# A two-layer streaming encoder step on one core: phases linked by two alternating semaphore sets instead of meetings, with three orders of filler work changed

## The chip, the core and the metric

The kernel runs on one core of one Trainium2 chip. The metric is the device time of one execution in microseconds (us), as a median of several runs. The engines are named as in the profile: PE is TensorE, ACT is ScalarE, DVE is VectorE, POOL is GpSimd, and SP is SyncE, which issues the DMAs of this kernel. A suffix q (PEq, SPq) is an engine's sequencer, PEld is the weight load of PE.

## What is computed

One inference step of a hybrid streaming encoder: 1024 new frames of one stream and 64 frames of a running stream (1088 tokens together), width 1024, two layers, all in 32-bit floats. Each layer normalizes and modulates its input, projects it once with a wide matrix, and divides the columns among three token mixers and the merge gates:

```
h      = modulate(rmsnorm(x), shift, scale)          # adaLN from c
proj   = h @ w_in                                     # columns split below
A      = retention(rotary(q), rotary(k), v, state)    # 4 heads, per-head decay, chunks of 64
B      = softmax(q k^T * hd^-0.5 + fq - fk, causal) v # "FoX": 8 heads, cumulative log forget gates, cache of 512
C      = gated_delta_rule(l2norm(silu(conv(q))), l2norm(silu(conv(k))), silu(conv(v)), g, beta, state)
y      = sum over branches of sigmoid(gate_br) * ((branch * silu(own gate)) @ w_branch[br])
x      = x + adaLN_gate * (y @ w_out)
```

After two layers there is a final RMSNorm. Outputs are the frames, and the new states and caches of the three mixers.

## The kernel before

The program is a row of 25 phases. Each layer has a norm phase, two retention phases (two heads each), four fox phases (two heads each), four delta phases (one head each) and a merge; the final norm is the last. Each phase is a block of its own (`nc.Block()`) with one instruction stream per engine, and ends in a meeting, `barrier()`, whose instructions the profile shows at L227: all engines come together, POOL clears the 57 semaphores that the phases share, and all go on. So every phase counts its semaphores from zero.

*Projections and turns.* A block is 128 columns of `w_in`. Block and activations are split into a high and a low part, and `three()` (L254 to L256) makes one product out of three matmuls. POOL splits a raw block into its parts (L308 high, L310 low), SP loads raw blocks some five ahead. A block takes three entries (364, 364 and 360 tokens) of 8 steps over the contraction; an entry fills one PSUM bank and is then evacuated by ACT (L290 or L296, both of which count `evacuated`). One step is a *turn*, three matmuls. `project` lets an entry start only when the bank that it takes has been evacuated: with `NB` banks, entry e waits for `evacuated >= e - NB + 1`. The generator `fill` yields the turns of a phase's projection, and `turns(fill, n)` puts n of them between the mixer's own small matmuls, whose operands other engines prepare in the meantime. Which turns stand where is written out by hand. The mixer's own matmuls write to other banks through `Ring`, whose `acquire` waits for the engine that takes a bank's last content.

*Retention.* 20 entries, three banks. Five `swap_halves` (L721), the v projection, then nine transposes of k in three groups (L745), nine pairs of score matmuls in three groups (L755), states (L768), outputs (L780, L783) and norm sums (L791), with turns between them.

*Fox.* 18 entries, two banks. First the 24 turns of the first block; then the first scores (L1078) and the transposes of v in three groups (L1097); the third group reuses a bank that DVE copies out at L1242, and that copy stands in DVE's order behind the first maxima (L1202), which need the decay matrix that POOL makes at L1060 out of a row that SP's DMA broadcasts from `scratch_fcum` (L1020). Then nine query blocks: scores, transposes of the probabilities (L1112), outputs (L1123, L1128). In layer 0 PE also makes modulation rows for later layers: `modulate` (L365) at some query blocks and `turn_rows` (L372) once, behind the last query block; DVE adds the bias (`add_bias`).

*Delta.* 18 entries, two banks (5 and 6), so entry e waits for e − 1 evacuations; 144 turns in all. The front: 24 turns; three sums of squares of k over the features (`sum_features`, L335), 4 turns, three sums for q, 10 turns, nine products of k with k (L1424), 2 turns, nine of k with q (L1424), 4 turns, nine transposes of k (L1417). Then six levels of small products (L1433) that invert a triangular matrix, with 30 turns between them, then a chain of nine steps over the chunks (L1522 to L1538) with 52 turns. Behind steps 5 and 7 and after the chain stand the three `part_sums` (L1443) of the output norm; the turns that are left follow. In the order of ACT the front is:

```
    roots_of(1, 0)
    roots_of(0, 3)
    act.wait_ge(act_took, 6)
    act.activation(rt[1][:, 0:TOK], rt[1][:, 0:TOK], ACT.Exp, scale=-0.5).then_inc(inverse, 1)
    kept(0)
...
    kept(1)
    silu(2, 3)
    for n in range(3):
        tiles_out(Kd, 12 + n, n, kdc)
    act.wait_ge(stored, 96)
    took = 2
```

`roots_of` makes the logarithms (L1573) of the sums, the first call those of k and the second those of q; `kept(m)` takes entry m + 3 (L290); `tiles_out` makes the scaled copies of the nine transposes (L1582); from `took` on the entries are taken between the levels and the steps of the chain.

Before it ACT makes taps, silus (L1555) and squares (L1559) of q and k. At the end of the phase DVE finishes the output in three parts, and SP stores them; its last wait is for all stores (block end at L1351).

*Merge.* It goes over 24 units (branch by output block); the gate blocks of the projection come first and fill four banks in turn before the first needs evacuating.

Of the kernel before, what the change touches and what calls it, by code (L numbers as in the profile page):

```python
# [22 lines left out]
F32 = mybir.dt.float32  # L23
# [5 lines left out]
P = 128  # L29
# [21 lines left out]
B = 32  # L51
# [72 lines left out]
def build(nc, A, O):  # L124
    with ExitStack() as ctx:
# [3 lines left out]
        sems = []  # L129

        def sem(name):
            s = ctx.enter_context(nc.semaphore(name))
            sems.append(s)
            return s

# [32 lines left out]
        branch_loaded = [sem(f"branch_loaded_{i}") for i in range(4)]  # L168
        x_loaded = [sem(f"x_loaded_{i}") for i in range(3)]
        x_stored = [sem(f"x_stored_{i}") for i in range(3)]  # L170
        gate_loaded = [sem(f"gate_loaded_{i}") for i in range(3)]
        o_next_loaded = [sem(f"o_next_loaded_{i}") for i in range(2)]
        params_loaded = sem("params_loaded")
        hist_loaded = sem("hist_loaded")
        o_loaded = sem("o_loaded")
        ada_loaded = [sem(f"ada_loaded_{i}") for i in range(4)]
        branch_hi = sem("branch_hi")
        branch_ready = sem("branch_ready")
        proj_done = sem("proj_done")
        diag_ready = sem("diag_ready")  # L180
        assembled = sem("assembled")
        evacuated = sem("evacuated")
        bank_ready = sem("bank_ready")
        act_took = sem("act_took")
        dve_took = sem("dve_took")
        stored = sem("stored")
        act_step = sem("act_step")
        dve_step = sem("dve_step")
        squares = sem("squares")
        squares_used = sem("squares_used")  # L190
        roots = sem("roots")
        inverse = sem("inverse")
        slot_used = sem("slot_used")
        h_scaled = sem("h_scaled")
        h_hi = sem("h_hi")
        h_ready = sem("h_ready")
        gates_raw = sem("gates_raw")
        tap_done = sem("tap_done")
        conv_done = sem("conv_done")
        silu_done = sem("silu_done")  # L200
        normed = sem("normed")
        decays = sem("decays")
        exps = sem("exps")
        level_mask = sem("level_mask")
        level_x = sem("level_x")
        state_ready = sem("state_ready")
        chain_pe = sem("chain_pe")
        rhs_ready = sem("rhs_ready")
        upd_ready = sem("upd_ready")
        out_pe = sem("out_pe")  # L210
        out_took = sem("out_took")
        out_done = sem("out_done")
        scores_pe = sem("scores_pe")
        beta_decay = sem("beta_decay")
        norm_sums = sem("norm_sums")
        logits = sem("logits")
        probs = sem("probs")
        merged = sem("merged")
        scaled = sem("scaled")
        gate_pe = sem("gate_pe")  # L220
        cleared = sem("cleared")
        nums = [s.num for s in sems]
        clear = range(min(nums), max(nums) + 1)
        assert len(clear) == len(sems)

        def barrier():
            nc.multi_engine_barrier(list(nc.engines), sems_to_clear=clear)  # L227

        def wait_own(eng, ins, count, s):

            count[0] += 1
            ins.then_inc(s, 1)
            eng.wait_ge(s, count[0])

        class Ring:

            def __init__(self, owners, first, banks):
                self.owners, self.first, self.banks = owners, first, banks

            def bank(self, n):  # L240
                return self.first + n % self.banks

            def acquire(self, pe, n):
                m = n - self.banks
                if m >= 0 and not isinstance(self.owners[m], str):
                    pe.wait_ge(*self.owners[m])
                elif m >= 0:
                    who = self.owners[m]
                    pe.wait_ge(act_took if who == "act" else dve_took,
                               sum(o == who for o in self.owners[:m + 1]))  # L250

        def three(pe, out, w_hi, w_lo, x_hi, x_lo, first, last):

            pe.matmul(out, w_hi, x_hi, start=first, stop=False)  # L254
            pe.matmul(out, w_hi, x_lo, start=False, stop=False)  # L255
            return pe.matmul(out, w_lo, x_hi, start=False, stop=last)  # L256

        def project(pe, e, first_bank, banks, slot):


            for s, (a, w) in enumerate(SEGS):
                if e + s >= banks:
                    pe.wait_ge(evacuated, e + s - banks + 1)
                for k in range(KC):
                    mm = three(pe, ps[:, first_bank + (e + s) % banks, 0:w], ws[:, slot, 0, k, :],
                               ws[:, slot, 1, k, :], hs[:, 0, k, a:a + w], hs[:, 1, k, a:a + w],
                               k == 0, k == KC - 1)
# [1904 lines left out]
```

## Time and profile before

| | |
|---|---|
| median of 3 runs | 3165.54 us (3164.61 to 3170.79) |
| profiled execution | 3164.03 us, of which the span from first to last instruction is 3162.3 us |
| mean granted TensorE clock | 0.978 |
| PE matmuls | 24012 instructions |
| DMA | 269.39 MB in 109956 packets |

In the profile's rows a timeline line has the start in us from the span's start, the duration, engine and line, operation, what is written and read, the count of instructions in the line, and in brackets how long the engine stood idle just before and what released it. Busy and idle times of PE are the ones to read first. The granted clock is a share of full speed: 1.0 is 2.4 GHz and 0.5 is 1.2 GHz, and a stretch's number is the mean.

### The profile page before, as it was taken

The numbers are of one execution on the slowest core, as the hardware profiler recorded it, in microseconds if no ns is written. First come the engines' busy times: TensorE is split into PE (matmuls) and PEld (weight loads), VectorE is DVE, ScalarE is ACT, GpSimd is POOL, SyncE is SP. The second block draws the span as 40 slices with busy tenths as digits, with TensorE's granted clock in tenths as the row PEclk, the third lists the DMA queues.
The fourth block names the chain that finished last, engine by engine and source line by source line (L and its number), as shares of the span: only waits on it lengthen the run. The fifth ranks groups of instructions, "written<-read, shape, count | busy, mean of one in ns | idle before, by whom it ended". The sixth has DMA issues, their size and how long they took to land. (4 is left out here: it accounts for less than half of the span.)

```text
span 3162.3 us, 55678 instructions
## 1 busy us (share of the span) xinstructions
PE 2948.4 (93%) x24012; PEld 2686.5 (85%) x24012; DVE 1106.3 (35%) x2568; ACT 1014.3 (32%) x1822; POOL 801.0 (25%) x520
## 2 busy tenths in 40 slices
PE   5999999999999999999959999999999999999996
PEld 3988888888898898999948888888888898899995
DVE  3312233233433433155143212343334433422632
ACT  4121423323434544222041214233325534531201
POOL 0221212212313323332212122212213313333320
PEclk7999999999999999999969999999999999999998
DMA  5111223223212211253222112212212211123323
GB/s 217 61 55 49 105 93 116 105 87 115 74 54 56 60 47 56 92 178 101 92 104 68 69 36 90 88 44 90 84 43 57 66 47 56 60 86 142 129 98 142
DMA packets 109956, 269.39 MB, mean 85 GB/s; under 512 B 38992, under 2 KB 45264, under 8 KB 108688
## 3 DMA queue, kind: packets, MB, share of 16 engines
q1 hardware_dynamic: 109712, 265.83, 24.8%
q8 instruction: 190, 3.11, 0.4%
q14 instruction: 54, 0.44, 0.1%
HBM read 208.20 MB, written 57.60 MB: 84 GB/s over the span
## 5 line engine op out<-in xcount | busy, mean ns | idle before, releaser
L254 PE MATMUL ps<-sb_h_split,sb_w_split 128*128 128x364 f32 (+1 forms) x3312 | 1180.7, 356 | 76.8 <-PEq L227 29.6
L256 PE MATMUL ps<-sb_h_split,sb_w_split 128*128 128x364 f32 (+1 forms) x3312 | 1092.7, 330 | 0.1
L255 PE MATMUL ps<-sb_h_split,sb_w_split 128*128 128x364 f32 (+1 forms) x3312 | 1092.6, 330 | 0.0
L254 PEld LDWEIGHTS ps<-sb_h_split,sb_w_split 128*128 128x128 f32 x3312 | 629.8, 190 | 145.4 <-issue 90.0
L308 POOL CAST sb_w_split<-sb_w_raw 128x1024 fp32r<-128x1024 f32 x154 | 166.4, 1081 | 1957.5 <-PE ps L256 1614.0
L255 PEld LDWEIGHTS ps<-sb_h_split,sb_w_split 128*128 128x128 f32 x3312 | 630.3, 190 | 6.4
L256 PEld LDWEIGHTS ps<-sb_h_split,sb_w_split 128*128 128x128 f32 x3312 | 627.4, 189 | 0.4 <-issue 0.4
L310 POOL TENSOR_TENSOR sb_w_split<-sb_w_raw,sb_w_split 128x1024 fp32r<-128x1024 f32 x154 | 370.5, 2406 | 12.3
L1230 DVE COPY sb_fox<-ps 128x512 f32<-128x512 f32 (+3 forms) x208 | 109.0, 541 | 290.4 <-PE ps L1112 289.9
L296 ACT ACTIVATE sb_raw_qk<-ps 128x364 f32<-128x364 f32 (+2 forms) x176 | 64.5, 393 | 347.0 <-PE ps L256 347.0
L1171 ACT ACTIVATE sb_fox<-sb_fox 128x128 f32<-128x128 f32 (+5 forms) x144 | 111.2, 773 | 98.2 <-DVE sb_fox L1208 98.0
L290 ACT ACTIVATE sb_fox<-ps 128x364 f32<-128x364 f32 (+1 forms) x96 | 45.5, 474 | 300.8 <-PE ps L256 300.8
L255 PE MATMUL ps<-sb_h_split,sb_wb_split 128*128 128x364 f32 (+1 forms) x384 | 125.9, 328 | 0.0
L256 PE MATMUL ps<-sb_h_split,sb_wb_split 128*128 128x364 f32 (+1 forms) x384 | 125.6, 327 | 0.0
L254 PE MATMUL ps<-sb_h_split,sb_wb_split 128*128 128x364 f32 (+1 forms) x384 | 125.4, 327 | 0.0
L1112 PE MATMUL ps<-sb_masks,sb_fox 128*128 128x128 f32 (+1 forms) x656 | 105.8, 268 | 0.0
L1202 DVE CUSTOM_DVE_ANT_0 sb_fox<-ps,sb_fox 128x128 f32<-128x128 f32 x144 | 39.9, 277 | 170.3 <-PE ps L1078 126.4
L1112 PEld LDWEIGHTS ps<-sb_masks,sb_fox 128*128 128x128 f32 (+1 forms) x656 | 80.0, 139 | 14.8 <-issue 7.4
L1078 PE MATMUL ps<-sb_fox 64*128 64x512 f32 (+3 forms) x448 | 88.8, 503 | 0.0
L1198 DVE CUSTOM_DVE_ANT_0 sb_fox<-ps,sb_fox 128x256 f32<-128x256 f32 (+7 forms) x128 | 86.3, 674 | 0.0
L1123 PE MATMUL ps<-sb_fox 128*64 128x128 f32 (+2 forms) x1312 | 84.6, 272 | 1.7 <-DVE sb_fox L1230 1.5
L1123 PEld LDWEIGHTS ps<-sb_fox 128*64 128x64 f32 (+1 forms) x1312 | 68.0, 136 | 19.5 <-issue 11.1
(263 smaller groups left out, 4332.0 us busy)
## 6 DMA issues: line engine op xcount, KB each, us to landing
sb_w_raw<-in_wblk SPq DMA_DIRECT2D x154, 512.0 KB, 5.5
sb_ada_fox<-in_adaw SPq DMA_DIRECT2D x32, 512.0 KB, 4.3
sb_raw_qk<-scratch_gate SPq DMA_DIRECT2D x24, 544.0 KB, 3.7
sb_fox<-scratch_fcum SPq DMA_DIRECT2D x8, 1600.0 KB, 7.2
sb_w_raw<-in_wbr SPq DMA_DIRECT2D x48, 256.0 KB, 4.2
scratch_gate<-sb_fox SPq DMA_DIRECT2D x16, 544.0 KB
scratch_gate<-sb_delta SPq DMA_DIRECT2D x16, 544.0 KB
sb_h_split<-scratch_o SPq DMA_DIRECT2D x16, 544.0 KB, 10.5
```

The lines of the kernel that those rows point to most:

```text
L254: pe.matmul(out, w_hi, x_hi, start=first, stop=False)
L255: pe.matmul(out, w_hi, x_lo, start=False, stop=False)
L256: return pe.matmul(out, w_lo, x_hi, start=False, stop=last)
L296: ins = act.activation(buf[:, u:u + w], ps[:, first_bank + e % banks, c:c + w], ACT.Copy)
L308: pool.tensor_copy(ws[:, to, 0], wraw[:, slot]).then_inc(split_hi, 1)
L310: pool.tensor_tensor(ws[:, to, 1], wraw[:, slot], ws[:, to, 0].bitcast(F32), ALU.subtract)\
L1078: mm = pe.matmul(ps[0:rows, 2 * h + a // 512, 0:w], qT[64 * h:64 * h + 64, P * t:P * t + rows], kT[64 * h:64 * h + 64, lo + a:lo + a + w], ...
L1112: mm = pe.transpose(ps[0:w, b, P * j:P * j + rows], lg[0:rows, h, (c + j) * P:(c + j) * P + w], ident[0:rows, 0:rows])
L1123: pe.matmul(ps[64 * h:64 * h + 64, b, 0:rows], V[0:w, vt, 64 * h:64 * h + 64], PT[0:w, h, P * c:P * c + rows], start=(c == 0), stop=(c == ...
L1171: act.activation(lg[0:rows, h, 0:n], lg[0:rows, h, 0:n], ACT.Exp, bias=mx[0:rows, s, 2:3], accum_out=mx[0:rows, s, 3:4])\
L1198: dve.tensor_tensor_reduce(out=lg[0:rows, h, 0:n], in0=src[:, 0:n], in1=fk[0:rows, h, lo:lo + n], scale=0.125, scalar=-3e38, op0=ALU.subtr ...
L1230: ins = dve.tensor_copy(dst[:, 0:full, 0:rows], src[:, 0:full, 0:rows])
```

## The change

All phases go into one block. There are two sets of the semaphores, and the phases use them in turn. An engine that finishes a phase counts its own semaphore `done` up (`leave`); before the next phase, the engines other than PE wait until all others have counted (`enter`), and POOL then clears the set that the finished phase used and counts `sets_cleared`. An engine enters a phase from the third on only when the set that it will use has been cleared. PE doesn't wait for the others at the start of a phase; it waits for `done["act"]` after three swaps in retention and after 8 turns in fox and delta (in the first fox phase of a layer at once). Before it leaves it waits for evacuations and other takers of its banks in the phase.

In delta's front the turns behind the first three sums go from 4 to 12, and of those behind the second three from 10 to 12, of which 4 stand between the second and the third of these sums. ACT takes entry 5 (`kept(2)`) before the levels. In fox's layer 0, 8 of the last turns go ahead of `turn_rows`. In retention the 4 turns behind each group of transposes go behind the group of scores instead, 12 there where 8 were.

The diff, without the changes of indentation and with repeated lines once:

```diff
+        done = {e: ctx.enter_context(nc.semaphore(f"done_{e}")) for e in ("sp", "pool", "pe", "act", "dve")}
+        sets_cleared = ctx.enter_context(nc.semaphore("sets_cleared"))
+        clears = []
+        def enter(eng, me, nr):
+            if nr >= 2:
+                eng.wait_ge(sets_cleared, nr - 1)
+            if nr >= 1 and me != "pe":
+                for who in done:
+                    if who != me:
+                        eng.wait_ge(done[who], nr)
+            if nr >= 1 and me == "pool":
+                eng.sem_clear(clears[(nr - 1) % 2])
+                eng.sem_inc(sets_cleared, 1)
+        def leave(eng, me):
+            if me == "pe":
+                eng.sem_inc(done[me], 1)
+            else:
+                eng.drain().then_inc(done[me], 1)
+        def phases_of(half):
...
-        def barrier():
-            nc.multi_engine_barrier(list(nc.engines), sems_to_clear=clear)
...
-        def sum_features(pe, ring, n, sq):
-            for s, (a, w) in enumerate(SEGS):
+            def sum_features(pe, ring, n, sq, segs=range(3)):
+                for s in segs:
+                    a, w = SEGS[s]
@@ each engine of each phase, at its start and its end
+                    enter(sp, "sp", nr)
+                    leave(sp, "sp")
@@ norm phase, PE's end
+                    pe.wait_ge(evacuated, 3)
+                    pe.wait_ge(gates_raw, 3)
@@ retention, PE
-                    for n in range(5):
-                        swap_halves(n)
+                    for m in range(5):
+                        if m == 3:
+                            pe.wait_ge(done["act"], nr)
+                        swap_halves(m)
...
                         mm.then_inc(bank_ready, 1)
-                        turns(fill, 4)
                     for n, (t, c) in enumerate(G3):
...
-                        turns(fill, 8)
+                        turns(fill, 12)
...
+                    pe.wait_ge(act_took, 12)
+                    pe.wait_ge(evacuated, 17)
@@ fox, PE
-                    turns(blocks(pe, L, [(0, first)], B0, NB), 25)
+                    if g == 0:
+                        pe.wait_ge(done["act"], nr)
+                    own = blocks(pe, L, [(0, first)], B0, NB)
+                    turns(own, 8)
+                    pe.wait_ge(done["act"], nr)
+                    turns(own, 17)
...
                     if todo:
+                        turns(fill, 8)
                         b = get(entry["mods"])
                         pe.wait_ge(dve_took, entry["m", 2 * rounds - 1] + 1)
                         turn_rows(pe, b, 0, mrow, len(todo)).then_inc(bank_ready, 1)
                     turns(fill, 120)
+                    pe.wait_ge(evacuated, 17)
+                    pe.wait_ge(dve_took, order + (1 if todo else 0))
@@ delta
-            front_turns = [24, 4, 10, 2, 4]
+                front_turns = [24, 12, 12, 2, 4]
...
-                    turns(fill, front_turns[0])
+                    turns(fill, 8)
+                    pe.wait_ge(done["act"], nr)
+                    turns(fill, front_turns[0] - 8)
                     pe.wait_ge(squares, 1)
                     sum_features(pe, ring, 0, sq[1])
                     turns(fill, front_turns[1])
                     pe.wait_ge(squares, 2)
-                    sum_features(pe, ring, 3, sq[0])
-                    turns(fill, front_turns[2])
+                    sum_features(pe, ring, 3, sq[0], range(2))
+                    turns(fill, 4)
+                    sum_features(pe, ring, 3, sq[0], range(2, 3))
+                    turns(fill, front_turns[2] - 4)
...
                     turns(fill, 120)
+                    pe.wait_ge(evacuated, 17)
+                    pe.wait_ge(out_took, 9)
+                    pe.wait_ge(state_ready, 9)
@@ delta, ACT
-                    took = 2
+                    kept(2)
+                    took = 3
@@ the end of the program
+        both = [phases_of(half) for half in range(2)]
+        order = [(0, (False, L)) if p == 0 else (p, (L, g)) if p < 4 else (4, (L,))
+                 for L in range(DEPTH) for p, count in enumerate((1, 2, 4, 4, 1)) for g in range(count)]
+        order.append((0, (True, None)))
+        with nc.Block() as block:
+            for nr, (p, what) in enumerate(order):
                 with ExitStack() as ph:
+                    both[nr % 2][p](block, *what, ph, nr)
```

## Rows read from the trace of the kernel before

**Rows 1.** The page's first part: busy time, share of the span, instructions.

```profile
PE 2948.4 (93%) x24012; PEld 2686.5 (85%) x24012; DVE 1106.3 (35%) x2568; ACT 1014.3 (32%) x1822; POOL 801.0 (25%) x520
```

**Rows 2.** Waits of PE: line, releaser, us in total, times, longest us.

```profile
PE ps L254 <- PEq L227: 29.6, 18, 1.7
...
PE ps L335 <- ACT sb_delta L1573: 14.1, 8, 1.8
...
PE ps L1417 <- DVE sb_delta L1739: 7.3, 8, 0.9
PE ps L1097 <- DVE sb_fox L1242: 7.2, 8, 1.7
...
PE ps L1424 <- DVE sb_delta L1719: 6.9, 16, 0.7
```

**Rows 3.** Timeline of one meeting, between two delta phases of layer 0.

```profile
1052.55 0.53 ACT L296 ACTIVATE sb_raw_qk<-ps 128x296 f32<-128x296 f32 x2 [3.51 <-PE ps L256]
...
1054.10 0.32 SPq L1354 DMA_DIRECT2D sb_delta<-scratch_g  x1
...
1054.15 0.40 PE L254 MATMUL ps<-sb_h_split,sb_w_split 128*128 128x364 f32 x1 [1.63 <-PEq L227]
```

**Rows 4.** Instructions of line L227: count, ns min/median/max, first and last start.

```profile
L227 POOLq EVENT_SEMAPHORE_RANGE_CLEAR  x25: 392/392/398, 110.6 to 3161.7; - x25
```

**Rows 5.** Timeline of ACT and PE in the front of a delta phase.

```profile
1063.15 1.11 ACT L1559 ACTIVATE sb_delta<-sb_delta 128x1088 f32<-128x1088 f32 x1
...
1066.19 1.99 PE L335 MATMUL ps<-sb_delta,sb_masks 128*128 128x364 f32 x6
...
1072.55 2.83 ACT L1573 ACTIVATE sb_delta<-ps,sb_consts 128x364 f32<-128x364 f32 x6
...
1073.16 0.87 PE L335 MATMUL ps<-sb_delta,sb_masks 128*128 128x360 f32 x2 [1.76 <-ACT sb_delta L1573]
...
1077.70 0.46 ACT L290 ACTIVATE sb_delta<-ps 128x364 f32<-128x364 f32 x1
...
1087.25 1.04 PE L1417 MATMUL ps<-sb_masks,sb_delta 128*128 128x128 f32 x8
...
1087.95 2.43 ACT L1582 ACTIVATE sb_delta<-ps,sb_delta 128x128 f32<-128x128 f32 x9 [2.58 <-PE ps L1417]
```

**Rows 6.** Timeline of SP and PE at the start of a fox phase, layer 1.

```profile
2033.15 0.32 SPq L1020 DMA_DIRECT2D sb_fox<-scratch_fcum  x1
...
2047.74 0.27 PE L1097 MATMUL ps<-sb_masks,sb_fox 128*64 128x128 f32 x1 [0.69 <-DVE sb_fox L1242]
```

**Rows 7.** Timeline of POOL and PE in a retention phase, layer 0.

```profile
233.12 2.34 POOL L310 TENSOR_TENSOR sb_w_split<-sb_w_raw,sb_w_split 128x1024 fp32r<-128x1024 f32 x1
...
265.62 0.43 PE L254 MATMUL ps<-sb_h_split,sb_w_split 128*128 128x364 f32 x1 [3.14 <-POOL sb_w_split L310]
...
272.34 1.16 PE L755 MATMUL ps<-sb_ret 64*128 64x128 f32 x16
```

**Rows 8.** Windows, PE: stretch, length, busy (groups), granted clock, DMA share, GB/s.

```profile
110.64:231.45 120.81, 116.04 (x749) 0.99 0.16 59
231.45:350.90 119.45, 114.68 (x749) 1.00 0.17 59
...
697.40:701.40 4.00, 4.00 (x16) 0.58 0.04 8
```

**Rows 9.** Timeline of ACT and PE near the end of three delta phases.

```profile
1155.62 0.47 ACT L1589 ACTIVATE sb_delta<-sb_delta 128x320 f32<-128x320 f32 x1
...
2471.28 0.70 PE L1443 MATMUL ps<-sb_delta,sb_masks 128*128 128x320 f32 x2
...
2585.86 0.70 PE L1443 MATMUL ps<-sb_delta,sb_masks 128*128 128x320 f32 x2
```

**Rows 10.** Line L1351, SP's end in two delta phases: ns, start.

```profile
L1351 SPq COMPARE_BRANCH  x1: 33/33/33, 2480.2 to 2480.2; - x1
...
L1351 SPq COMPARE_BRANCH  x1: 32/32/32, 2593.1 to 2593.1; - x1
```

More of the change, by code:

```diff
@@ L167, in build @@
         split_ready = ctx.enter_context(nc.semaphore("split_ready"))
[L168 to L203, printed above, removed]
@@ L218, in build @@
[L218 to L224, printed above, removed]
-        def barrier():
-            nc.multi_engine_barrier(list(nc.engines), sems_to_clear=clear)
[L229 to L258, printed above, removed]
-            for s, (a, w) in enumerate(SEGS):
[L262 to L267, printed above, removed]
-                    if k == KC - 1:
-                        mm.then_inc(proj_done, 1)
-                    yield
@@ L272, in await_split @@
-        def await_split(eng, L, b):
-            eng.wait_ge(split_ready, L * N_BLOCKS + b + 1)
-        def blocks(pe, L, todo, first_bank, banks):
-            for e, b in todo:
-                await_split(pe, L, b)
-                yield from project(pe, e, first_bank, banks, (b + 1) % 2)
-        def turns(gen, n):
-            for _ in range(n):
-                next(gen, None)
-        def take(act, e, first_bank, banks, dst, func=ACT.Copy):
-            w = dst.shape[-1]
-            act.wait_ge(proj_done, e + 1)
-            act.activation(dst, ps[0:dst.shape[0], first_bank + e % banks, 0:w], func).then_inc(evacuated, 1)
@@ L331, in sum_features @@
-        def sum_features(pe, ring, n, sq):
-            for s, (a, w) in enumerate(SEGS):
-                ring.acquire(pe, n + s)
-                pe.matmul(ps[:, ring.bank(n + s), 0:w], ones, sq[:, a:a + w],
-                          start=True, stop=True).then_inc(bank_ready, 1)
-        def row(name, idx):
-            ap = A[name] if name in A else O[name]
-            return ap[idx]
-        def Q4(ap):
-            return ap.rearrange("p (t c) -> p t c", c=P)
-        def flat(ap):
-            return ap.rearrange("p t c -> p (t c)")
@@ L350, in small_of @@
-        def small_of(m):
-            return small[:, m:m + 1, :].to_broadcast([P, NTILE, B])
-        def tiles_of(mask):
-            return mask.unsqueeze(1).to_broadcast([P, NTILE, P])
-        G3 = [(0, 4), (4, 4), (8, 1)]
-        def modulate(pe, bank, w_, n):
-            for r in range(2):
-                for j in range(4):
-                    mm = pe.matmul(ps[32 * j:32 * j + 32, bank, 0:P * n], cT[:, 2 * j + r, :], w_[:, :, 2 * j + r, :],
-                                   start=(r == 0), stop=(r == 1))
-            return mm
@@ L369, in turn_rows @@
-        def turn_rows(pe, bank, at, rows, n):
-            for i in range(n):
-                mm = pe.matmul(ps[:, bank, at + 2 * i:at + 2 * i + 2], rows[:, P * i:P * i + P], pick,
-                               start=True, stop=True)
-            return mm
-        def add_bias(dve, L, n, count, src):
-            return dve.tensor_tensor(modT[:, L, n:n + count, :], src.rearrange("p (n c) -> p n c", c=2),
-                                     adab[:, L, n:n + count].unsqueeze(2).to_broadcast([P, count, 2]), ALU.add)
```

678 lines of the change are left out of this document (410 added, 268 removed).

## The prediction

> **What bounds the kernel now.** I read the page's first part, the waits of TensorE (PE), and then the timeline of one phase of each kind. PE is busy 93% of the span and no other engine 36% [rows 1], so time is gained or lost only where PE idles or runs at a lower clock. The page's second part shows PE at 9 in all but a few of forty slices, the norm phases, which the change leaves alone inside. The waits [rows 2] name what is left to win: 29.6 us at the first projection matmul behind the meeting (L227), at most 1.7 us each, and in delta's front 14.1 us on ScalarE (ACT) and 14.2 us on VectorE (DVE). A turn is one step of the projection that PE uses as filler: three matmuls, 0.5 us; 24 turns are a block of 12 us.
>
> The profiled execution took 3164.0 us (span 3162.3), 1.5 us under the median of the three runs. The sum is made against 3164.0 and 1.5 is put back at the end. About 0.2% (6.3 us) is what a measurement of this kernel can tell from no change.
>
> **A link instead of a meeting.** [Rows 3] are one meeting: ACT takes the phase's last entry at 1052.55 + 0.53 = 1053.08; SP's next DMA is issued at 1054.10, 1.02 us on; PE starts at 1054.15 after 1.63 us idle, and with the pipelining of a matmul lost I call it 1.8. Of the 1.02 us, 0.39 is POOL's clear [rows 4]. After the change PE runs on and wins up to 1.8 us per link, wherever it finds work that needs no other engine. The others still wait for ACT's end; the trace has no such hand-over of four signals and a drain, so I bound it between 0 and the meeting's whole 1.02. I take 0.2, the value of the nearest single wait: in delta ACT's copies begin 0.7 behind the start of PE's transposes, of which the first four take 0.5 [rows 5]. Other engines thus start 1.02 − 0.2 = 0.8 us earlier against ACT's end; POOL, which still clears, 0.8 − 0.39 = 0.4. What PE is given depends on what comes next:
> - Merge (2 links): its own blocks fill four banks, 16 us of turns, before PE wants anything evacuated; the whole lead stays: 2 × 1.75 = 3.5.
> - Fox (8): PE reaches its third v transpose after 25 turns and then waits for the V copy, the end of a chain that starts with SP's broadcast DMA at 2033.15 and releases PE 14.6 us later [rows 6]; all eight already wait there (7.2 us in all [rows 2]). PE's lead only lengthens this wait; the phase is as much earlier as SP: 0.82 each, 6.6. If the chain hides more than it seems, 1.8 each, 14.4.
> - Retention (4): after five swaps PE needs the second block, whose split on POOL ends 233.12 + 2.34 = 235.46 [rows 7], just when PE comes. So POOL's 0.4 counts: 4 × 0.43 = 1.7.
> - Norm of layer 1, final norm, end of the program: SP's and ACT's 0.8 each, 2.4.
>
> Together 14.2. The new waits of PE at a phase's end are for evacuations that ACT made turns before; the wait for ACT's drain stands behind 8 turns (4.0 us) in fox and delta, behind three swaps in retention. ACT needs 0.5 us after PE's last matmul [rows 3], so both cost nothing; without the turns each would cost about that 0.5.
>
> **Retention.** At 265.62 PE has waited 3.14 us for POOL's split, as the first four turns stand behind the first transposes [rows 7]. Moved behind the scores, the other five transposes (about 0.4 us) and the first sixteen score matmuls (1.16 at 272.34, minus overlap 1.09) go into the wait: 1.5 each, 4 × 1.5 = 6.0. The same turns come later, nothing is added. Bounds: 0, if the scores wait for DVE's rotation; 3.1 each, were the whole stall filled.
>
> **The clock.** [Rows 8]: two retention phases of the same 749 PE groups took 116.04 us busy at a granted clock of 0.99 and 114.68 at 1.00: a stretch at the lower level (1.2 GHz) behind the stall costs 1.36, here 1.4. Behind layer 0's fox turn_rows (L372) the granted clock is 0.58 over 4 us. Two of four retention stalls and two of four such fox phases show it. Half the stall remains in retention and turn_rows gets turns on both sides, so I count all four as saved: 4 × 1.4 = 5.6 (bounds 0 and 5.6).
>
> In those four fox phases turn_rows comes 4 us later, six turns (3.0 us) and ACT's 0.53 before the phase's last evacuation. Behind it DVE has a bias addition and a product over 64 columns, and SP one store. I cost it at nothing, under those 3.5 us; if SP's store took as long as delta's 7.2 (below), 3.7 at each of four links would be lost.
>
> **Delta's front.** All times from PE's start, 1054.15. Work after the change: 24 turns to 12.04; three sums and 4 turns to 15.9; 8 more turns to 19.9; two sums and 4 turns to 23.1; the third sum ends at 23.9. Next is entry 5 of the projection, and it needs a bank: two banks serve the entries, so entry 3 must have been taken by ACT (kept(0), L290). In ACT's order kept(0) stands behind all six logarithms (L1573) and the exponential. The sixth logarithm needs the very sum that was put off. In [rows 5] the six logarithms end at 1072.55 + 2.83 = 1075.38 and kept(0) at 1077.70 + 0.46 = 1078.16, 2.78 later; with one logarithm before that (2.83/6 = 0.47) and 0.2 for the hand-over it is 3.45. So PE idles from 23.9 to 27.3 in each of eight phases. Before, in the same stretch, it waits 1.76 at the last sum [rows 5], 0.17 and 0.69 at the products and 0.90 at the transposes (the eightfold sums in [rows 2]): 3.5. The new stall replaces the old ones: 8 turns to 31.4, products to 33.4, 2 turns, products to 36.5, 4 turns, transposes to 39.75 with 54 turns spent. Before, the transposes end at 35.1 with 44 turns, which is 40.1 with 54. Gain 0.4 per phase. Bounds: 3.5 if kept(0) is no obstacle; −3.4 if the old stalls stay as well.
>
> kept(2) stands behind the nine scaled copies, which take 2.43 us and begin 0.7 after PE's first transpose [rows 5], so it is done at 39.3 + 2.43 + 0.47 = 42.2. PE wants that bank at turn 57, 40.85: loss 1.4. Put there it covers the next entry, so the later order of ACT shifts by one entry: at the chain's step 7 the last part's square (0.47 [rows 9]) stands behind an entry that PE finishes just then (turn 136), whose copy is 0.4. PE's part sum there is late by 1.1 (bounds 0 and 1.1).
>
> The front now takes ten turns out of the phase's 144, so the tail behind the last part sum shrinks from 18 turns to 8. SP's chain of stores does not shrink: the sum at 2585.86 [rows 9] and SP's end at 2593.1 [rows 10] are 7.2 us apart, as in six of eight phases; at 2471.28 and 2480.2 it is 8.9. PE's phase now ends 0.4 + 4.1 = 4.5 after the sum. All engines wait for SP, so the next phase's DVE and ACT start 7.2 + 0.2 − 4.5 = 2.9 behind PE. In a delta phase the first square ends at 1063.15 + 1.11, that is 10.11 after PE's start, and PE wants it at 12.04: 1.9 spare. Loss 2.9 − 1.9 = 1.0, and 1.8 and 2.7 for the slower stores; over the six delta to delta links 8.5 with both slow ones (bounds: 0 and 6 × 2.7 = 16). (PE itself starts 1.8 earlier, as it runs through the link; that is the next sum's first term.)
>
> Per phase then: link −1.8, front −0.4, kept(2) +1.4, part sum +1.1, sum +0.3; × 8 = 2.4 lost; with the 8.5 it is 10.9. Each new 3.45 us stall may cost the clock; retention's stalls of 3.14 did in two of four [rows 7, 8], so half: 4 × 1.4 = 5.6 (bounds 0 and 11.2).
>
> On this the Trainium skill ("TensorE: Matmul & The Clock Gate", section "HAM oscillation — how this bites in real kernels") says that matmul bursts with idle waits between them start again at the lower clock. By it all eight stalls would cost the 1.4, and the sum would come to 3.7 instead of 9.3. The trace bears it out at two of four such stalls.
>
> **Sum.** 14.2 + 6.0 + 5.6 − 10.9 − 5.6 = 9.3 us gained: 3164.0 − 9.3 = 3154.7, and with 1.5 for the median 3156. The likeliest's own range is 3149 to 3161, from the clock (±5.6) and half of the store bounds.
>
> **Rivals.** *The filler fits (0.20).* ACT takes entry 3 early enough, PE is not held, and the ten turns fill the old stalls: the transposes end at 36.5 instead of 40.1. A phase then wins 1.8 + 3.6 − 1.4 − 1.1 = 2.9, and no clock is lost: 14.2 + 6.0 + 5.6 + 8 × 2.9 − 8.5 = 40.5, about 3125. For it: the stalls exist [rows 2]. Against: ACT's order in the code, and two banks.
>
> *Every stall costs the clock (0.20).* 8 × 1.4 = 11.2 instead of 5.6: gain 3.7, about 3162. For it: 0.58 after a short run of small matmuls [rows 8]; against: two of four.
>
> *The hand-over costs what the meeting did (0.15), the other side.* Each engine drains and waits for four semaphores, POOL clears besides; if that takes 1.0 instead of 0.2, the fox, retention and norm links give nothing (−10.7) and delta's next phases start 0.8 later still (6 × 0.8 = 4.8): 9.3 − 15.5 = −6.2, about 3172. Each tenth costs 1.9, so it decides at 0.7, where the gain is gone. For it: 1.02 less the clear leaves 0.63 [rows 3, 4]; against: the single wait's 0.2 [rows 5].
>
> My own account has 0.45. Faster by over 0.2% (under 3159.2): of mine 0.38, the filler's 0.20, and 0.03 of the clock's: 0.61. Slower (over 3171.9): 0.07 of the hand-over's, 0.04 of stores and clock together: 0.11. The rest, 0.28, is no change. For eight in ten the range reaches from just under the filler's 3125 to 3168, short of the hand-over's 3172.
>
> **What would show it.** No wait on L227 at L254. In delta, PE waits of about 3.4 us, eight times, at a projection matmul for ACT's copy, and of 1.4 after the transposes; the waits on L1719 and L1739 gone; 1.1 at the last part sum (L1443); about 1.0 at the first squares' sum at six links, with SP's end 2.9 behind PE's start. Retention's stall 1.6 in place of 3.1; clock 1.0 behind fox's turn_rows; fox's third transpose still waiting, longer by 1. Wrong if kept(0) is taken early enough, if SP's end comes before PE's, or if the engines start 0.7 us or more after the last signal.

## The result and the profile after

The changed kernel takes 3184.95 us (median of 4 runs, 3184.54 to 3188.82) where the kernel before takes 3165.07 (4 runs): the ratio is 1.0063, with a 95% interval of 1.0045 to 1.008. It is some 20 us slower; 3156 and a gain were forecast, with a range up to 3168. The profiled execution took 3188.82 us, with a span of 3187.0.

First the page's first part, then PE's waits (line, releaser, us in total, times, longest), of the changed kernel. Lines moved: the projection is L276 to L278 now, ACT's evacuations L312 and L318, POOL's split L330 and L332, the sums of squares L358 (the squares themselves L1633), fox's transposes of v L1150 and delta's part sums L1508.

```profile
PE 2962.8 (93%) x24012; PEld 2701.9 (85%) x24012; DVE 1146.2 (36%) x2568; ACT 1014.2 (32%) x1822; POOL 811.0 (25%) x520
```

```profile
PE ps L276 <- ACT sb_delta L312: 38.6, 16, 3.4
...
PE ps L1150 <- DVE sb_fox L1302: 13.1, 8, 2.7
PE ps L276 <- ACT sb_delta L318: 12.5, 8, 1.7
...
PE ps L276 <- POOL sb_w_split L332: 10.7, 8, 1.5
PE ps L358 <- ACT sb_delta L1633: 9.0, 6, 2.0
...
PE ps L1508 <- ACT sb_delta L1663: 7.4, 8, 0.9
```

Against [rows 1] PE does the same 24012 matmuls in 14.4 us more, and the mean granted clock is 0.974 against 0.978; and DVE does the same 2568 instructions in 39.9 us more, which nothing in the change asks for. Against [rows 2] the meeting's 29.6 us, the waits on L1719 and L1739 and those for the logarithms are gone, and waits for ACT in delta have come: 38.6 and 12.5 for a bank, 9.0 for the first squares, 7.4 at the last part sum.

Where the time went is read by stage. The windows of the changed kernel run from a stage's first matmul to the next one's: stretch, length, PE busy, groups, granted clock, DMA share, GB/s. In order: retention, fox, delta and merge of layer 0, norm, and retention, fox, delta and merge of layer 1.

```profile
111.77:347.11 235.34, 229.29 (x1499) 1.00 0.17 60
347.11:816.06 468.95, 460.54 (x3437) 1.00 0.31 106
816.06:1292.46 476.40, 434.77 (x5169) 0.98 0.19 53
1292.46:1593.72 301.26, 288.44 (x1729) 0.99 0.36 127
1593.72:1684.21 90.49, 59.99 (x264) 0.76 0.20 76
1684.21:1919.58 235.37, 229.31 (x1500) 1.00 0.17 60
1919.58:2363.66 444.08, 436.62 (x3116) 1.00 0.22 74
2363.66:2847.70 484.04, 438.36 (x5170) 0.98 0.18 52
2847.70:3152.08 304.38, 291.41 (x1729) 0.98 0.36 126
```

The same windows of the kernel before, two of nine, delta in layer 0 and 1:

```profile
826.85:1283.06 456.21, 427.30 (x5168) 1.00 0.20 56
...
2368.13:2824.17 456.04, 427.18 (x5168) 1.00 0.19 56
```

The others before are 240.26 and 240.28 (retention), 475.37 and 446.56 (fox), 304.73 and 302.73 (merge), 93.50 (norm). So, change against before, with the forecast by stage beside it:

| stage | measured, us | forecast, us |
|---|---|---|
| retention, 4 phases | −9.8 | −10.5 (link 1.7, scores 6.0, clock 2.8) |
| fox, 8 phases | −8.9 | −9.4 (link 6.6, clock 2.8) |
| merge and norm of layer 1 | −4.8 | −4.3 (3.5 and 0.8) |
| delta, 8 phases | +48.2 | +16.5 (10.9 and the clock's 5.6) |

Outside delta the sums by stage came as forecast. (A window ends where PE starts the next stage, so PE's lead at a link, up to 1.8 us, stands in the stage before it; merge by itself has −1.8 and norm −3.0.) Delta lost three times what I gave it: 18.7 us of it are PE busy longer (434.77 and 438.36 against 427.30 and 427.18) at a clock of 0.98 where it was 1.00, and 29.5 are idle.

The front of the third delta phase of layer 0 after the change, PE in the timeline, shows three waits where I had two, at the first sums, at entry 4 and at entry 5:

```profile
1067.85 2.10 PE L358 MATMUL ps<-sb_delta,sb_masks 128*128 128x364 f32 x6 [1.71 <-ACT sb_delta L1633]
...
1075.60 0.43 PE L276 MATMUL ps<-sb_h_split,sb_w_split 128*128 128x364 f32 x1 [1.66 <-ACT sb_delta L318]
...
1080.91 0.77 PE L358 MATMUL ps<-sb_delta,sb_masks 128*128 128x360 f32 x2
1085.11 0.67 PE L276 MATMUL ps<-sb_h_split,sb_w_split 128*128 128x360 f32 x1 [3.43 <-ACT sb_delta L312]
```

The last is the stall of entry 5, forecast at 3.45. The first was forecast at 1.0. The second, at entry 4, is not in my account: entry 4 needs entry 2's evacuation, and that stands in ACT's order behind the second squares, which come late.

```profile
1074.02 1.11 ACT L1633 ACTIVATE sb_delta<-sb_delta 128x1088 f32<-128x1088 f32 x1
1075.03 0.51 ACT L318 ACTIVATE sb_delta<-ps 128x296 f32<-128x296 f32 x2
```

One more wait, 1.33 behind the transposes, was forecast at 1.4. What makes the first two long stands in the timeline of DVE, POOL and SP in the same phase:

```profile
1054.90 0.33 SPq L1441 DMA_DIRECT2D scratch_o<-sb_delta  x1
1057.16 0.17 DVE L1768 COPY sb_raw_qk<-sb_delta_small 128x3 f32<-128x3 f32 x1 [2.29 <-SPq L182]
1057.67 1.04 POOL L330 CAST sb_w_split<-sb_w_raw 128x1024 fp32r<-128x1024 f32 x1 [17.99 <-POOLq L174]
1058.79 2.41 POOL L332 TENSOR_TENSOR sb_w_split<-sb_w_raw,sb_w_split 128x1024 fp32r<-128x1024 f32 x1
1059.59 2.69 DVE L1783 SCALAR_TENSOR_TENSOR sb_delta<-sb_raw_qk,sb_delta_small,sb_delta 128x1024 f32<-128x1024 f32 x1 [1.61 <-ACT sb_delta L1623]
1067.68 2.36 POOL L332 TENSOR_TENSOR sb_w_split<-sb_w_raw,sb_w_split 128x1024 fp32r<-128x1024 f32 x1
1067.71 3.41 DVE L1783 SCALAR_TENSOR_TENSOR sb_delta<-sb_raw_qk,sb_delta_small,sb_delta 128x1024 f32<-128x1024 f32 x1
```

PE started at 1054.00; DVE starts at 1057.16, 3.16 later, behind SP's last store (I had 2.9). POOL starts half a microsecond behind DVE, as it clears first. DVE's convolution step of 1024 columns takes 1.28 us by itself; here the first takes 2.69 and ends at 1062.28, which is 1.08 behind the end of POOL's split (1061.20), and the fifth takes 3.41 and ends at 1071.12, 1.08 behind the end of POOL's next split (1070.04). So it is in three of the eight phases; in the other five a step takes 1.94 to 2.08, and POOL's split 3.24 to 3.27 in place of 2.4. In the kernel before the first step overlaps POOL's split by 0.3 us only, and the second split (its CAST starts at 1066.42) comes when the convolutions are done:

```profile
1055.24 2.42 POOL L310 TENSOR_TENSOR sb_w_split<-sb_w_raw,sb_w_split 128x1024 fp32r<-128x1024 f32 x1
...
1057.36 1.38 DVE L1706 SCALAR_TENSOR_TENSOR sb_delta<-sb_raw_qk,sb_delta_small,sb_delta 128x1024 f32<-128x1024 f32 x1 [1.53 <-ACT sb_delta L1549]
```

It too ends 1.08 behind POOL's 1057.66. So DVE's step waits out POOL's split. The Trainium skill ("SBUF — State Buffer", section "Who interferes with whom") has the rule: a VectorE instruction with two inputs in SBUF contends with a GpSimd instruction that reads SBUF, as its second input comes through a port that the two share; the port is an exclusive lock, and the order of issue decides who blocks. These rows agree with it, 1.08 three times.

### The profile page after: what moved, and what is told of

The parts are those of the page before. It is cut to its first block and busy times, and to the rows that moved or that the text cites. A ratio compares the mean times of both kernels' runs of the same rounds, so it can differ in the third digit from the quotient of the medians.

```text
span 3187.0 us, 55477 instructions
## 1 busy us (share of the span) xinstructions
PE 2962.8 (93%) x24012; PEld 2701.9 (85%) x24012; DVE 1146.2 (36%) x2568; ACT 1014.2 (32%) x1822; POOL 811.0 (25%) x520
## 5 line engine op out<-in xcount | busy, mean ns | idle before, releaser
L276 PE MATMUL ps<-sb_h_split,sb_w_split 128*128 128x364 f32 (+1 forms) x3312 | 1187.0, 358 | 94.4 <-ACT sb_delta L312 38.6
L278 PE MATMUL ps<-sb_h_split,sb_w_split 128*128 128x364 f32 (+1 forms) x3312 | 1098.5, 332 | 0.0
L276 PEld LDWEIGHTS ps<-sb_h_split,sb_w_split 128*128 128x128 f32 x3312 | 634.1, 191 | 167.1 <-issue 59.4
L330 POOL CAST sb_w_split<-sb_w_raw 128x1024 fp32r<-128x1024 f32 x154 | 167.5, 1088 | 1916.2 <-PE ps L278 1532.9
L278 PEld LDWEIGHTS ps<-sb_h_split,sb_w_split 128*128 128x128 f32 x3312 | 632.2, 191 | 0.0
L332 POOL TENSOR_TENSOR sb_w_split<-sb_w_raw,sb_w_split 128x1024 fp32r<-128x1024 f32 x154 | 378.6, 2459 | 12.3
L318 ACT ACTIVATE sb_raw_qk<-ps 128x364 f32<-128x364 f32 (+2 forms) x176 | 64.6, 393 | 330.1 <-PE ps L278 330.1
L312 ACT ACTIVATE sb_fox<-ps 128x364 f32<-128x364 f32 (+1 forms) x96 | 45.5, 474 | 297.0 <-PE ps L278 297.0
L278 PE MATMUL ps<-sb_h_split,sb_wb_split 128*128 128x364 f32 (+1 forms) x384 | 125.6, 327 | 0.0
L276 PE MATMUL ps<-sb_h_split,sb_wb_split 128*128 128x364 f32 (+1 forms) x384 | 125.4, 327 | 0.0
L1783 DVE SCALAR_TENSOR_TENSOR sb_delta<-sb_raw_qk,sb_delta_small,sb_delta 128x1024 f32<-128x1024 f32 x96 | 104.7, 1138 | 14.0 <-ACT sb_delta L1623 12.9
L276 PE MATMUL ps<-sb_w_split,sb_h_split 128*128 128x256 f32 x288 | 82.2, 285 | 4.7 <-POOL sb_w_split L332 4.7
## 6 DMA issues: line engine op xcount, KB each, us to landing
sb_h_split<-scratch_o SPq DMA_DIRECT2D x16, 544.0 KB, 10.1
```

Of the source, the lines that this page charges most:

```text
L318: ins = act.activation(buf[:, u:u + w], ps[:, first_bank + e % banks, c:c + w], ACT.Copy)
L330: pool.tensor_copy(ws[:, to, 0], wraw[:, slot]).then_inc(split_hi, 1)
L332: pool.tensor_tensor(ws[:, to, 1], wraw[:, slot], ws[:, to, 0].bitcast(F32), ALU.subtract)\
L1783: ins = dve.scalar_tensor_tensor(c[:, b:b + w], u[:, a + j:a + j + w], cw[:, 4 * x + j:4 * x + j + 1], c[:, b:b + w], ALU.mult, ALU.add)
```

## The experiments

My theory after the result: delta loses by three causes, ACT's order at entry 5, DVE against POOL, and SP's late store, and the clock falls behind each long stall. The main rival: the links cost by themselves in delta. Every ratio below is against the kernel before on the same chip.

**The old front on links.**

```diff
-front_turns = [24, 12, 12, 2, 4]
+front_turns = [24, 4, 10, 2, 4]
-sum_features(pe, ring, 3, sq[0], range(2)); turns(fill, 4); sum_features(pe, ring, 3, sq[0], range(2, 3))
-turns(fill, front_turns[2] - 4)
+sum_features(pe, ring, 3, sq[0])
+turns(fill, front_turns[2])
-kept(2)
-took = 3
+took = 2
```

> The links, fox and retention as in the changed kernel, but delta's front, its sums and ACT's order there as before the change. Theory (the new front is guilty: ACT's order holds PE, the clock falls behind that stall, and the shorter tail leaves the others late): the gain outside delta, about 23 us, stays, and each delta phase is no longer than before, up to 1.8 us shorter through its link; 3128 to 3142 us. Rival (the links themselves cost in delta, whatever its front): delta stays some 3 us longer in each phase, about 3165 us or more.

Measured: 3158.53 us, ratio 0.9959 (0.9944 to 0.9973), between the two. The new front is 0.0104 worse than the old one on links, but the old one isn't free of loss either. Its timeline:

```profile
1059.53 2.08 DVE L1780 SCALAR_TENSOR_TENSOR sb_delta<-sb_raw_qk,sb_delta_small,sb_delta 128x1024 f32<-128x1024 f32 x1
...
1060.62 3.25 POOL L332 TENSOR_TENSOR sb_w_split<-sb_w_raw,sb_w_split 128x1024 fp32r<-128x1024 f32 x1
...
1066.29 0.57 PE L358 MATMUL ps<-sb_delta,sb_masks 128*128 128x364 f32 x1 [3.03 <-ACT sb_delta L1631]
...
1070.01 0.97 PE L358 MATMUL ps<-sb_delta,sb_masks 128*128 128x360 f32 x1 [1.94 <-ACT sb_delta L1645]
```

With the long tail DVE starts only 0.89 behind PE, and still the last step of the convolutions runs into POOL's second split, and PE waits 3.03 for the second squares, where the kernel before had no wait. Behind these two stalls the clock is 0.50 (the window below: stretch, length, busy, groups, clock, DMA share, GB/s):

```profile
1070.00:1074.20 4.20, 4.20 (x12) 0.50 0.75 264
```

Over all eight delta phases PE is idle as long as before (0.1 us more) and busy 15.6 us longer, at a granted clock of 0.97 where it was 1.00: here the loss is the clock's.

**ACT takes entry 3 first.**

```diff
 roots_of(1, 0)
+kept(0)
 roots_of(0, 3)
 act.wait_ge(act_took, 6)
 act.activation(rt[1][:, 0:TOK], rt[1][:, 0:TOK], ACT.Exp, scale=-0.5).then_inc(inverse, 1)
-kept(0)
```

> The changed kernel, with ACT taking entry 3 (kept(0)) ahead of the second three logarithms instead of behind the exponential. Theory (the 3.43 us stall is ACT's order, and the clock falls because of it): the stall at entry 5 goes, about 2 us per phase stay won after the waits for the normalized k and q that come behind it, and most of the clock's losses behind it go (8 times some 1.5); 3157 to 3169 us. Rival (the way of the third sum through logarithm, table load and exponential sets the time, and PE would wait for the normalized k instead): under 5 us gained, 3180 us or more, the clock falling as before.

Measured: 3155.0 us, ratio 0.9952 (0.9936 to 0.9968): 0.0111 less than the changed kernel, some 35 us. PE's wait on ACT's L312 falls from 38.6 to 3.0 us:

```profile
PE ps L276 <- ACT sb_delta L312: 3.0, 14, 0.3
```

The stretch where the 3.43 us stall was, first in the changed kernel (its 3 us behind the stall) and then here:

```profile
1085.10:1088.10 3.00, 2.99 (x10) 0.51 0.08 31
```

```profile
1071.00:1075.50 4.50, 4.44 (x26) 1.00 0.93 365
```

PE runs on at 1.00. The delta stretches are busy 429.81 and 432.90 us here, 10.4 less together than after the change. That ACT then still needs a table load and the exponential costs 0.41 us in place of 3.43, and PE waits for DVE at the transposes again, 0.91 us a phase as in the kernel before. The theory holds, and the gain is larger than expected; the 1.33 behind the transposes also shrank to 0.27, as ACT is ahead from there on.

**POOL's split behind the convolutions.**

```diff
+pool.wait_ge(conv_done, 2)
 pool.wait_ge(proj_done, 3)
 split_block(pool, L, first + 2)
```

> The changed kernel, with POOL's split of delta's third block held until DVE has finished the convolutions of k and q. Theory (DVE's and POOL's work of over 1 us slow each other when they run together, and the late start in delta brings them together): the convolution's 1.28 us rows come back from 3.41 us, the second square is some 2 to 3 us earlier, PE's wait of 1.6 at the turn behind ACT's third evacuation goes; 13 to 20 us gained, 3165 to 3172 us. Rival (that wait is only the late start): the convolution's rows stay long or the wait stays, within 5 us of the changed kernel's 3185.

The split of the third block is POOL's second in the phase. Measured: 3173.9 us, ratio 1.0013 (1.0004 to 1.0023), 0.0050 or some 16 us less than the changed kernel by the ratios, 11 by the medians. The wait of 12.5 us on ACT's L318 is gone, and DVE's steps from the second on take 1.28 us in all eight phases; only the first is still 2.7. The mean of the 48 steps of 1024 columns, before, after and here, is 1299, 1728 and 1522 ns. So the theory holds, and the late start alone doesn't make the wait.

**The new front on meetings.** The kernel before, with delta's front (its turns, the third sum and `kept(2)`) changed as in the change and nothing else.

> The kernel before, with its meetings, and delta's new front alone (12 turns behind each three sums, the third sum of q put off, kept(2) ahead of the levels). Theory (the front is guilty by itself): per phase the new stall replaces the old ones (-0.4), kept(2) costs 1.4, the last part sum 1.1 and the clock some 1.5, together 3.6, times 8 is 29 us; about 3190 us, without a wait at the first sum and without the wait of 1.6 behind ACT's third evacuation, since all engines start together. Rival (the links are guilty, the front is good): at or under 3165 us.

Measured: 3235.45 us, ratio 1.0204 (1.0189 to 1.022), twice the loss expected. The front is guilty by itself. Two of its waits:

```profile
PE ps L254 <- PEq L227: 46.0, 18, 3.7
PE ps L254 <- ACT sb_delta L290: 38.7, 16, 3.4
```

The stalls at entry 5 and behind the transposes are the same, 38.7 in all. As expected, PE waits neither at the first sums nor at entry 4, so these two waits come only with the links. What I had left out here is the meeting: with a tail of 8 turns SP's stores end after PE, and in a meeting PE waits them out, 46.0 us against 29.6 [rows 2], and the clock falls behind that wait as well (behind one of 3.69 us a matmul of the projection takes 0.51 us in place of 0.33). In delta PE idles 38.0 us more than before and is busy 23.0 us longer, where I had 12 for the clock.

**The two mends together.** Both edits, entry 3 first and the split behind the convolutions.

> Both single mends of the changed kernel together: ACT takes entry 3 ahead of the second three logarithms, and POOL's split of delta's third block waits for the convolutions. Theory (two causes that add: ACT's order at entry 5, and DVE against POOL): PE's wait behind ACT's third evacuation (12.7 us with the first mend alone) goes and nearly all of it is gained over the 3155 us of the first mend: 3140 to 3148 us. Rival (one stall in two guises: whichever is mended, the other wait takes its place): within 4 us of 3155 us.

Measured: 3142.17 us, ratio 0.9933 (0.9914 to 0.9952). The 12.7 us wait at entry 4 is gone, and the longest wait left in delta's front is that at the first sum (9.0 us over six phases). By the ratios the second mend adds 0.0019, some 6 us, by the medians 13, by the delta stages of the two profiled executions 20 (908.7 us against 928.7):

```profile
815.97:1269.66 453.69, 429.19 (x5169) 1.00 0.20 55
2340.72:2795.69 454.97, 430.29 (x5169) 1.00 0.19 55
```

The ratios by themselves, with these intervals, don't tell the second mend's gain from nothing. That the causes add rests on the traces: the one wait goes without another in its place, and delta is shorter.

**POOL clears later.** In addition, in delta POOL's `enter` leaves out the clear, and it follows the first split:

```diff
-enter(pool, "pool", nr)
+enter(pool, "pool", nr, clear=False)
 split_block(pool, L, first + 1)
+clear_last(pool, nr)
```

> As the two mends together, and in delta POOL clears the finished phase's set after its first split instead of before it, so that the split starts with DVE's first work. Theory (DVE's first row of the convolution is long, 2.7 instead of 1.38 us, since POOL, half a microsecond late through its clear, is still splitting): that row comes back to under 2 us, the first square is about 1 us earlier, and PE's wait at the first sum (9.0 us at six phases) shrinks to some 2 us or less; 5 to 8 us less than the two mends. Rival (that row is long for another reason, such as ACT's taps or SP's loads): the row stays at 2.7 us and the time within 2 us of the two mends.

Measured: 3133.12 us, ratio 0.9904 (0.9889 to 0.9918), 0.0029 or some 9 us less. The first step takes 1.37 us in six phases, 2.36 in the two behind fox, and the mean step is 1338 ns. The wait at the first sum is 5.6 us at six phases, down from 9.0; the expected 2 was too low, and what is left I put down to SP's late store. The 9 us are more than the mend explains: between the two profiled executions delta is only 1.9 us shorter (906.8 against 908.7), and the rest of their 6 us lies in stages that the edit leaves alone.

**The old front, kept apart from POOL.** The old front on links, with these two edits of POOL.

> Delta's front as before the change, on links, with POOL's third split held behind the convolutions and its clear behind the first split. Theory (the old front on links lost 3.0 us per phase at the second squares' sum and the clock behind it, 3158 us, only because DVE and POOL ran into each other): that wait goes, the clock stays up in delta, and the time is 25 to 35 us lower, 3122 to 3133 us. Rival (the old front simply has too few turns there on links): the wait of 3.0 us stays, 3150 us or more.

Measured: 3132.12 us, ratio 0.9904 (0.9887 to 0.9921), 0.0055 or some 17 us less than with the old front alone, less than the 25 expected, to a time within the expected bounds. The wait of 3.0 at the second squares is gone: 3.4 us in all eight phases, from 24.2, first with the old front alone and then here:

```profile
PE ps L358 <- ACT sb_delta L1631: 24.2, 8, 3.0
```

```profile
PE ps L362 <- ACT sb_delta L1637: 3.4, 8, 0.4
```

What stays is 17.8 us for the logarithms at the third sum, where the kernel before has 14.1 [rows 2], and the clock still fell five times in delta.

**ACT's order at two more places.**

```diff
 silu(2, 3)
+kept(2)
 act.wait_ge(exps, 2)
 for n in range(3):
     tiles_out(Kd, 12 + n, n, kdc)
 act.wait_ge(stored, 96)
-kept(2)
...
+if i == 8:
+    part_square(2)
 while took < turns_before[i + 1] // 8 - 3:
     kept(took)
     took += 1
```

and `part_square(2)` left out where it stood.

> As the run with the later clear, and two more places in ACT's order in delta: kept(2) ahead of the copies of the transposes instead of behind them, and the last part's square ahead of the entry that stood before it. Theory (the 1.33 us at the turn behind the transposes and the 0.92 us at the last part sum are ACT's order, as predicted): both waits go, 8 times 2.2 us, 12 to 18 us less than the run with the later clear, with no new wait over 0.5 us in the front. Rival (the transposes' copies or the levels wait instead): under 5 us less.

Measured: 3118.08 us, ratio 0.9856 (0.9842 to 0.9871), some 15 us less. The 7.4 us at the part sums are gone. The 1.33 of kept(2) had already shrunk with the first mend, so that its own part is 2.2 us of waits (3.4 to 1.2). This version beats both kernels: 46 us or 1.4% under the one before, on the same chip. Its delta stretches:

```profile
816.09:1262.25 446.16, 426.88 (x5170) 1.00 0.20 56
2333.53:2778.11 444.58, 427.93 (x5169) 1.00 0.20 56
```

Busy as before the change, at a clock of 1.00, and shorter by 10.1 and 11.5. Against the run with the later clear delta is 16.1 us shorter, 10.9 of it idle; the other 5.1 are PE's busy time, at a clock of 1.00 in both, and no row here shows where they come from.

**The links alone.** Delta's front, retention's turns and fox's turn_rows as before the change, so that only the links are left.

> The links alone: the changed kernel with delta's front, retention's turns and fox's turn_rows as before the change. Theory (the links win 14 us outside delta and lose it again in delta, where DVE and POOL run into each other and the clock falls behind the wait for the second squares): retention about 2 us and fox about 0.7 us per phase longer than in the changed kernel, delta about as long as with the old front on links; the time within 8 us of the kernel before. Rival (the prediction's account: 14.2 us outside delta and 1.8 us at each of eight delta links): 3135 to 3145 us.

Measured: 3174.46 us, ratio 1.0024 (1.0013 to 1.0034). By the medians that is 7 us above the kernel before on this chip, within the expected 8. By stage against before: retention +5.8, fox −7.5, merge −2.9, norm −2.5, delta +16.5 us. The links by themselves gain nothing: delta loses as with the old front above, and the clock fell in all four retention phases where before it fell in two, as the 3.1 us stall is still there:

```profile
PE ps L276 <- POOL sb_w_split L332: 17.2, 8, 3.1
```

Whether the links make the clock fall oftener in retention isn't shown: in the run of the new front on meetings, with retention as before, it fell in two phases too, but in another two. Against the changed kernel a retention phase is 3.9 us longer (2 expected) and a fox phase 0.2 (0.7 expected).

## Why the prediction was wrong

*The links' hand-over: right.* DVE's first work follows SP's drain by 0.1 us (a drain at 1057.08, DVE at 1057.16, and so at all six links from delta to delta); I had 0.2 and a rival at 1.0. The stages outside delta came to what the sum says, in part by luck, as the parts differ. In fox no stretch at the lower clock follows turn_rows any more, but PE's lead makes it wait longer at the third transpose, 13.1 us against 7.2, and in two phases the clock falls behind that wait instead, as in the window below, behind a wait of 2.67 us (stretch, length, busy, groups, granted clock, DMA share, GB/s). So the clock gave nothing there, with two such stretches before and two after, and the links more than 6.6: in the run of the links alone PE idles 8.3 us less in fox than before.

```profile
596.50:599.90 3.40, 3.28 (x11) 0.51 0.64 183
```

*Retention: right in size.* The stall is 1.5 at most where it was 3.1, the clock is 1.00 in all four phases, −9.8 us against −10.5. The links alone show that the moved turns, not the links, gave it: there PE idles only 0.5 us less in retention than before, where I had 1.7, since it waits another 1.15 us a phase for POOL's split of the second block.

*The front: the stall at entry 5 was right, and its neighbour was missed.* 38.6 us in 16 waits are the 3.45 and the 1.4 that I had for kept(0) and kept(2) (measured 3.43 and 1.33 to 1.40), and taking entry 3 first removed nearly all. The step that failed is "Next is entry 5 of the projection, and it needs a bank": entry 4 starts earlier, at turn 33, and needs entry 2's evacuation, which in ACT's order stands behind the second squares. With 12 turns ahead of the second sums in place of 4 this comes up before PE asks for those squares: 12.5 us. On meetings the same front has no such wait, so it takes the early entry and the late squares together.

*The delay in delta: right in its cause, too small in its effects.* SP's store is behind by what I said, and the first sums wait 9.0 us in all (8.5 forecast). That these meet is luck in part: with POOL's clear moved 5.6 us are left, so 3.4 came from a collision that my sum doesn't have. I took "the first square ends … 10.11 after PE's start" as if only its start moved. The link also moves POOL against DVE, by its own clear at the start, and DVE against PE, whose 24th turn sets off POOL's second split. A collision costs DVE up to 2.1 us (3.41 against 1.28), and the second squares, with the evacuation behind them, come late. Three runs show it: holding POOL's second split removed the wait at entry 4 with the new front, the same together with the later clear removed the wait at the second squares with the old front, and the later clear shortened the wait at the first sums.

*The clock: the step "so half: 4 × 1.4" failed.* Delta was busy 18.7 us longer, not 5.6. The granted clock fell at all eight stalls of 3.43 us, in two of these phases for twice as long and in two more a second time. In the stretches at the lower level PE is busy 38.1 us in delta, where the kernel before has no such stretch; at half the clock up to 19 us of that are lost, an estimate. With the two mends there is no stretch at the lower clock in delta either, and PE is still busy 5.0 us longer than before (859.5 against 854.5), with ACT's order changed at two more places 0.3; so at least 13.7 of the 18.7 hang on the stalls, and up to 5 may be something other than the clock. This is the rival that I gave 0.20, and it was right about the mechanism, not the size. That is also what the Trainium skill's rule ("TensorE: Matmul & The Clock Gate", section "HAM oscillation — how this bites in real kernels") says of bursts with idle waits between, and eight of eight stalls here agree with it; the trace before, with two of four, was a poor guide.

*Together.* Of the 31.7 us by which delta missed the forecast, 13.1 are PE's longer busy time (18.7 − 5.6), most of it the clock, 12.5 the wait at entry 4, and 2.7 waits of the chain's steps (L1595), which the new front has on meetings too. The remaining 3.4 are terms that I had a little wrong: the stall at entry 5 (27.4 us in eight phases) and the old waits that it replaces (28.3) nearly cancel, where I counted 3.2 won, and delta's eight links save 13.2 us of waits, not 14.4; the other differences cancel.

What stays open: the first sums' last 5.6 us, which I put down to SP's store without a run that moves the store; and the up to 5 us of PE's busy time in delta that stand at a clock of 1.00.

## What to carry to other kernels

Before filling a stall with work from a generator, list for every bank that the filler needs which evacuation frees it and what stands ahead of that evacuation in its engine's order: here one line moved in ACT's order was worth 1.1%, and the same turns went from a loss to a gain. When a meeting is taken away, the engines' starts shift against each other; look for pairs that slow each other (here DVE with two operands in SBUF and POOL) and missed each other by luck: in the kernel before, POOL's second split starts at 1066.42, just when DVE's convolutions end. A stall of PE can cost the stretch at the lower clock behind it besides its length; here that took most of 18.7 of the 48.2 us lost in delta.

## What the runs showed of the hardware

A DVE step of 1.28 us over two SBUF operands waited for the end of POOL's instruction: it ended 1.08 us behind POOL's end in the three cases shown, and took up to 3.41 us; with the old front on links POOL's split in its turn took 3.25 us in place of 2.4. An order by semaphores alone, over five engines, cost 0.1 us from the last signal in the hand-over read above, where a meeting took 1.02 from ACT's last evacuation to SP's next DMA [rows 3]. POOL's clear (0.4 us) moved POOL half a microsecond behind DVE; with the clear behind the split the waits at the first sums fell from 9.0 to 5.6 us. A stall of 3.43 us brought the granted clock from 1.00 to 0.50 in eight of eight cases in the changed kernel, one of 3.14 us in two of four before and in four of four with the links alone.
